# Expert products of a decoder step: from three fp32r products on split weights to plain fp32 products on column tiles

## What is computed

```python
D_MODEL, N_EXPERTS, TOP_K, D_FF_EXPERT = 1024, 8, 2, 3584

def swiglu(h, w_gate_up, w_down):
    a, b = jnp.split(h @ w_gate_up, 2, axis=-1)
    return (jax.nn.silu(a) * b) @ w_down

def moe_swiglu(h, w_router, b_router, w_gate_up, w_down):
    logits = (h @ w_router).astype(jnp.float32) + b_router.astype(jnp.float32)
    top_val, top_idx = lax.top_k(logits, TOP_K)
    top_w = jax.nn.softmax(top_val, axis=-1)
    gates = jnp.sum(jax.nn.one_hot(top_idx, N_EXPERTS) * top_w[..., None], axis=-2)
    y = jnp.zeros_like(h)
    for e in range(N_EXPERTS):
        y = y + gates[..., e:e + 1] * swiglu(h, w_gate_up[e], w_down[e])
    return y
```

## Time and profile before

| | |
|---|---|
| runs of the kernel | 1690.48, 1697.03 and 1693.4 us, median 1693.4 |
| span of the profiled execution, first to last instruction | 1690.0 us |
| TensorE, VectorE, ScalarE busy | 95%, 75%, 64% of the span |
| mean granted clock of TensorE | 0.975 |
| read and written in memory | 522.56 MB and 17.48 MB |

### The profile page before, as it was taken

One profiled execution on the slowest core, in us unless ns is written; L12 is line 12 of the kernel. 1 busy time (PEld: TensorE's weight loads), 2 busy tenths in 40 slices (PEclk: granted clock), 3 DMA queues, 4 the chain that ended last, 5 costly groups with the idle time before them and its releaser, 6 DMA issues.

```text
span 1690.0 us, 25152 instructions
## 1 busy us (share of the span) xinstructions
PE 1603.4 (95%) x9180; PEld 1304.9 (77%) x9180; DVE 1266.3 (75%) x1446; ACT 1074.4 (64%) x1302; POOL 84.2 (5%) x121
## 2 busy tenths in 40 slices
PE   7999899999997888999999999999999999999993
PEld 3983778899896465788788888888888888888883
DVE  4653654454677244899898998998998998998993
ACT  4633444443554443787777877777877777877771
POOL 2011010000024000000000000000000000000001
PEclk9999899999999899999999999999999999999996
DMA  9559578875576987999999999999999999999972
GB/s 348 182 214 352 193 244 290 298 249 182 212 250 242 374 295 271 349 361 368 376 377 376 380 371 378 373 375 376 376 374 378 374 374 383 368 368 386 380 281 103
DMA packets 239603, 540.96 MB, mean 320 GB/s; under 512 B 5931, under 2 KB 28585, under 8 KB 239538
## 3 DMA queue, kind: packets, MB, share of 16 engines
q1 hardware_dynamic: 229202, 504.42, 82.2%
q0 software_dynamic: 9392, 32.39, 5.2%
q10 hardware_dynamic: 944, 3.26, 0.5%
HBM read 522.56 MB, written 17.48 MB: 320 GB/s over the span
## 4 chain that ended last, share of the span: by engine, by line
PE 73%; issue 16%; DVE 4%; DMA 4%; ACT 1%; POOL 0%; SPq 0%; ACTq 0%; DVEq 0%; POOLq 0%
PE psum L780 21%; PE psum L781 21%; PE psum L782 21%; PE psum L699 2%; DMA ring<-in_ada_w 2%; PE psum L1181 1%; DVE w_lo L1722 1%; DMA ring<-in_moe_w_gate_up 1%; PE psum L889 1%; PE psum L692 1%; DVE ring L2061 1%; PE psum L1024 1%; PE psum L1175 1%; PE psum L860 0%; DMA h<-q_scratch 0%
## 5 line engine op out<-in xcount | busy, mean ns | idle before, releaser
L2221 DVE TENSOR_TENSOR w_lo<-ring,w_hi 128x1024 fp32r<-128x1024 f32 x672 | 812.6, 1225 | 79.7 <-ACT w_hi L1643 66.5
L1643 ACT CAST w_hi<-ring 128x1024 fp32r<-128x1024 f32 x672 | 704.8, 1053 | 204.4 <-PE psum L782 186.8
L780 PE MATMUL psum<-w_hi,xe_hi 128*128 128x512 f32 x896 | 359.5, 401 | 3.0 <-DVE w_lo L2221 3.0
L781 PE MATMUL psum<-w_lo,xe_hi 128*128 128x512 f32 x896 | 355.0, 396 | 0.0
L782 PE MATMUL psum<-w_hi,xe_lo 128*128 128x512 f32 x896 | 354.8, 396 | 0.0
L1722 DVE TENSOR_TENSOR w_lo<-ring,w_hi 128x1024 fp32r<-128x1024 f32 (+1 forms) x132 | 161.9, 1236 | 145.8 <-ACT w_hi L1322 145.7
L780 PE MATMUL psum<-hh,w_hi 128*128 128x264 f32 x864 | 254.4, 294 | 16.7 <-DVE w_lo L1722 9.3
L781 PE MATMUL psum<-hl,w_hi 128*128 128x264 f32 x864 | 248.2, 287 | 0.0
L782 PE MATMUL psum<-hh,w_lo 128*128 128x264 f32 x864 | 248.0, 287 | 0.0
L1322 ACT CAST w_hi<-ring 128x1024 fp32r<-128x1024 f32 (+1 forms) x132 | 135.9, 1034 | 106.8 <-PE psum L782 69.0
L780 PEld LDWEIGHTS psum<-w_hi,xe_hi 128*128 128x128 f32 x896 | 169.0, 189 | 42.4 <-DVE w_lo L2221 3.9
(11 more groups left out here) (373 smaller groups left out, 1403.6 us busy)
## 6 DMA issues: line engine op xcount, KB each, us to landing
ring<-in_moe_w_gate_up SPq DMA_DIRECT2D x112, 2048.0 KB, 9.6
ring<-in_moe_w_down SPq DMA_DIRECT2D x56, 2048.0 KB, 9.0
ring<-in_ada_w SPq DMA_DIRECT2D x24, 2048.0 KB, 9.1
ring<-in_ffn_w_gate_up SPq DMA_DIRECT2D x22, 1024.0 KB, 7.7
ring<-in_gla_w_in SPq DMA_DIRECT2D x6, 2048.0 KB, 10.8
ring<-in_kv_ada_w SPq DMA_DIRECT2D x4, 2048.0 KB, 8.9
ring<-in_ffn_w_down SPq DMA_DIRECT2D x4, 2048.0 KB, 8.6
ring<-in_kv_w SPq DMA_DIRECT2D x4, 2048.0 KB, 11.3
```

Source lines behind the costliest of these rows:

```text
L780: eng.matmul(to, wh, ah, start=start, stop=False)
L781: eng.matmul(to, wh, al, start=False, stop=False)
L1643: eng.copy(unit(w_hi, kind, n), quarter(ring[(BASE + j // 4) % RING], kind, j % 4)).then_inc(S["hi_ready"], 1)
L2221: eng.tensor_tensor(unit(w_lo, kind, n), quarter(ring[(BASE + j // 4) % RING], kind, j % 4), unit(w_hi, kind, n), ALU.subtract).then_inc(S ...
```

## The change

The products of the experts are plain fp32 on the loaded tiles. `w_hi`, `w_lo`, `xe_hi`, `xe_lo`, `at_hi` and `at_lo` are no longer used in the sparse branch, nor are the casts and subtractions. `CAP` is 96. A block of 1024 weight columns is four pieces of 256: in three rounds, all 96 tokens meet pieces 0, 1 and 2, on array columns 0 to 63 and 64 to 95; in the same round 32 of the tokens meet piece 3 on array columns 96 to 127. So after three rounds the fourth piece is done too. Its outputs stand in partitions 96 to 127, which the transposes (`turn`), the copy out (`gate_rows`) and the stores (`send_outputs`) take apart again. The ring has six tiles: two in the place of `w_hi` and `w_lo`, one new, and the three old ones. SyncE loads a tile again when TensorE is done with it (`tile_used`). Twelve of the 14 gate and up tiles are now 512 rows x 1024 columns, two stay 1024 x 512. The loop holds two experts (`PAIR`). `y_e` is copied out at the end of an expert instead of at the start of the next, by ScalarE. The dense branch is changed to the new tiles in the same way.

```diff
-CAP = 128
-
-TURN_ROWS_AT, SPLIT_ROWS_AT, GATE_ROWS_AT = 66, 70, 40
+CAP = 96
+ROUNDS = 3
+FULL, REST = 256, 128
+E_RING = 6
+PAIR = 2
...
+PER_BODY = PAIR * PER_E
+UP_TILES = 14
+GROUPS = ((0, 4, FULL), (4, 4, FULL), (8, 4, FULL), (12, 2, REST))
+GROUP_CHUNKS = (8, 8, 8, 4)
+CHUNK0 = (0, 8, 16, 24)
+TURN_AT = {4: 0, 8: 1, 12: 2, 14: 3}
+ROWS_TURN_AT = 18
...
+        e_ring = [stage.enter_context(nc.sbuf_tensor(f"e_ring{i}", [P, TILE], F32)) for i in range(2)]
...
+        e_ring += [st_sb(stage, "e_ring2", [P, TILE])] + [ring[slot] for slot in OLD_SLOTS]
...
-        xe_hi = st_sb(gathered, "xe_hi", [P, KC, CAP], F32R)
-        xe_lo = st_sb(gathered, "xe_lo", [P, KC, CAP], F32R)
-        at_hi = st_sb(gathered, "at_hi", [P, FEC, CAP], F32R)
-        at_lo = st_sb(gathered, "at_lo", [P, FEC, CAP], F32R)
-        silu_e = st_sb(gathered, "silu_e", [CAP, 512])
-        act_e = st_sb(gathered, "act_e", [CAP, 512])
-        y_e = st_sb(gathered, "y_e", [CAP, D])
-        y_g = st_sb(gathered, "y_g", [CAP, D])
+        xe = st_sb(gathered, "xe", [P, KC, CAP])
+        picks = st_sb(gathered, "picks", [P, NE * TT, CAP], F32R)
+        at = st_sb(gathered, "at", [P, FEC, CAP])
+        silu_e = st_sb(gathered, "silu_e", [P, ROUNDS * FULL])
+        act_e = st_sb(gathered, "act_e", [P, ROUNDS * FULL])
+        y_e = st_sb(gathered, "y_e", [P, D])
+        y_g = st_sb(gathered, "y_g", [P, D])
...
+                if i < 12:
+                    s, half = i % 4 // 2, i % 2
+                    c = s * FE + i // 4 * D
+                    src = up[expert, half * 512:(half + 1) * 512, c:c + D].rearrange("(k p) c -> p k c", p=P)
+                elif i < UP_TILES:
+                    c = (i - 12) * FE + 3 * D
+                    return cols8(dst), up[expert, :, c:c + 512].rearrange("(k p) c -> p k c", p=P)
...
+            eng.wait_ge(S["kv_stored"], 16 * 6)
+            eng.wait_ge(S["unit_used"], NU)
+            for j in range(E_RING):
+                if j >= E_RING - RING:
+                    eng.wait_ge(*read_out(*STREAM[LAST_IN[j - (E_RING - RING)]]))
...
-                    value = eng.snap(it * (4 * PER_E) + (NU + 4 * (j - RING) + 4))
-                    eng.wait_ge(S["lo_ready"], value)
...
+                    value = eng.snap(it * PER_BODY + (j - E_RING + 1))
+                    eng.wait_ge(S["tile_used"], value)
...
+            def send_outputs(to, of):
+                to = to[:, :]
+                strip = of[CAP:P, 0:ROUNDS * FULL].rearrange("p (r c) -> p r c", r=ROUNDS)
+                eng.dma_start(to[:, 0:ROUNDS * FULL], of[0:CAP, 0:ROUNDS * FULL]).then_inc(S["y_e_sent"], 16)
+                eng.dma_start(to[:, ROUNDS * FULL:D].rearrange("(r p) c -> p r c", p=STRIP), strip).then_inc(S["y_e_sent"], 16)
...
+                def turn(g):
+                    bank0, width = 3 * (g % 2), GROUPS[g][2]
+                    for c in range(GROUP_CHUNKS[g]):
+                        r, lo = c * P // width, c * P % width
+                        to = pb[bank0 + c // 4][:, c % 4 * CAP:(c % 4 + 1) * CAP]
+                        if r < ROUNDS:
+                            last = eng.transpose(to, act_e[0:CAP, r * width + lo:r * width + lo + P], ident[0:CAP, 0:CAP])
+                            continue
+                        for s in range(ROUNDS):
+                            last = eng.transpose(to[:, s * STRIP:(s + 1) * STRIP], act_e[CAP:P, s * width + lo:s * width + lo + P],
+                                                 ident[CAP:P, CAP:P])
                     last.then_inc(S["turned"], 1)
 
+                def rounds(outs, tokens, j, k, width, first, stop, opens=(0, 1, 2)):
+
+                    for r in range(ROUNDS):
+                        start = first and r in opens
+                        w, rest = expert_cols(j, k, r * width, width), expert_cols(j, k, ROUNDS * width, width)
+                        eng.matmul(outs[r][0:64, :], tokens[:, 0:64], w, start=start, stop=stop, skip_group_check=True)
+                        eng.matmul(outs[r][64:CAP, :], tokens[:, 64:CAP], w, start=start, stop=stop, skip_group_check=True)
+                        last = eng.matmul(outs[r][CAP:P, :], tokens[:, r * STRIP:(r + 1) * STRIP], rest, start=start, stop=stop,
+                                          skip_group_check=True)
+                    return last
+
+                down_outs = [psum[:, (6 * 512 + r * FULL):(6 * 512 + (r + 1) * FULL)] for r in range(ROUNDS)]
...
+                with eng.Fori(0, NE // PAIR) as it:
+                    for e in range(PAIR):
+                        def of(per, n):
+                            return it * (PAIR * per) + (e * per + n)
+
+                        eng.wait_ge(S["xe_act_kept"], of(1, 1))
+                        eng.wait_ge(S["xe_dve_kept"], of(1, 1))
+                        for i in range(PER_E):
+                            j = e * PER_E + i
+                            if i < UP_TILES:
+                                g = min(i // 4, 3)
+                                first, n_tiles, width = GROUPS[g]
+                                if i == first and g == 1:
+                                    eng.wait_ge(S["rows_placed"], 5)
+                                if i == first and g >= 2:
+                                    eng.wait_ge(S["at_act_kept"], of(4, g - 1))
+                                    eng.wait_ge(S["at_dve_kept"], of(3, g - 1))
+                                expert_landed(eng, it, j)
+                                s = (i - first) * 2 // n_tiles
+                                outs = [pb[3 * (g % 2) + r][:, s * FULL:s * FULL + width] for r in range(ROUNDS)]
+                                ks = range(KC) if n_tiles == 2 else range((i - first) % 2 * 4, (i - first) % 2 * 4 + 4)
+                                for n, k in enumerate(ks):
+                                    last = rounds(outs, xe[:, k, :], j, n, width, k == 0, k == KC - 1)
+                            else:
+                                i0 = i - UP_TILES
+                                if i0 == 0:
+                                    eng.wait_ge(S["y_kept_free"], of(1, 1))
+                                    eng.wait_ge(S["at_act_kept"], of(4, 3))
+                                    eng.wait_ge(S["at_dve_kept"], of(3, 3))
+                                if i0 == 6:
+                                    eng.wait_ge(S["at_act_kept"], of(4, 4))
+                                expert_landed(eng, it, j)
+                                for k in range(4):
+                                    c = 4 * i0 + k
+                                    last = rounds(down_outs, at[:, c, :], j, k, FULL, c == 0, c == FEC - 1, opens=(0, 2))
+                            last.then_inc(S["tile_used"], 1)
+                            if i in TURN_AT:
+                                eng.wait_ge(S["gate_up_kept"], of(4, TURN_AT[i] + 1))
+                                turn(TURN_AT[i])
+                            if i == ROWS_TURN_AT:
+                                eng.wait_ge(S["expert_rows"], it * (PAIR * 16) + (e * 16 + 32))
+                                turn_rows()
...
+                with eng.Fori(0, NE // PAIR) as it:
+                    for e in range(PAIR):
+                        def of(per, n):
+                            return it * (PAIR * per) + (e * per + n)
+
+                        for g, (first, n_tiles, width) in enumerate(GROUPS):
+                            eng.wait_ge(S["tile_used"], of(PER_E, first + n_tiles))
+                            if g >= 1:
+                                eng.wait_ge(S["gate_up_kept"], of(4, g))
+                            gates = psum[:, 3 * (g % 2) * 512:3 * (g % 2 + 1) * 512].rearrange("p (r c) -> p r c", r=ROUNDS)
+                            eng.activation(silu_e[:, 0:ROUNDS * width].rearrange("p (r c) -> p r c", r=ROUNDS), gates[:, :, 0:width],
+                                           ACT.Silu).then_inc(S["e_silu"], 1)
+                            eng.wait_ge(S["turned"], of(4, g + 1))
+                            eng.copy(at[:, CHUNK0[g]:CHUNK0[g] + 4, :], pb[3 * (g % 2)][:, 0:4 * CAP]
+                                     .rearrange("p (k c) -> p k c", k=4)).then_inc(S["at_act_kept"], 1)
+                        keep_rows(of(2, 3))
+                        eng.wait_ge(S["tile_used"], of(PER_E, PER_E))
+                        eng.wait_ge(S["y_kept_free"], of(1, 1))
+                        eng.copy(y_e[:, 0:ROUNDS * FULL], psum[:, 6 * 512:6 * 512 + ROUNDS * FULL]).then_inc(S["y_e_kept"], 1)
...
+                keep_rows(2)
+                eng.wait_ge(S["last_spread"], 48)
+                with eng.Fori(0, NE // PAIR) as it:
+                    for e in range(PAIR):
+                        def of(per, n):
+                            return it * (PAIR * per) + (e * per + n)
+
+                        for g, (first, n_tiles, width) in enumerate(GROUPS):
```

(27 more changed lines are left out.)

297 lines of the change are left out of this document (99 added, 198 removed).

## The result

The changed kernel takes 3104.5 us (median of four runs, 3101.8 to 3106.6) where the kernel before takes 1693.2 us (1690.5 to 1697.0) beside it: a ratio of 1.832, 95% interval 1.829 to 1.835. The forecast was 1648 us. The first rival, different widths that don't share the array, had been priced at 3040 us.

What follows compares the result with a forecast made beforehand. TensorE was taken to set the pace, transfers close behind. It starts near 676, plus 3 and 8 x 115.7 us gives 1604.6; the end stage of 38 plus 1 gives a span of 1644, a time of 1648 us (1620 to 1685).

Steps and rivals of the forecast that it cites:

- The first rival: Expert products: the 64-wide product runs alone, the 32-wide pair after it, 1.10 us a round, 3040 us; chance 0.34.
- Part (2): Expert products on TensorE: 64-, 32- and 32-wide tiles work at once, 0.43 us a round, 108.4 us against 117.9 us.
- the exclusion: Expert products: column tiles of different widths don't share the array, 3040 us; chance 0.34.
- the rival's lower end: Expert products, widths not sharing: a change of shape costs 0.09 us, 1.04 us a round, 2905 us at the least.
- part (3): TensorE's transposes: 5.4 us against 3.9, plus 14 changes of tile shape at 0.1 us each, 1.4 us.
- Part (1): VectorE and ScalarE: 88 and 103 us of casts and subtractions per expert go, beside TensorE's work; gain by itself nothing.
- Part (4): Waits added on TensorE for tiles and activations: cost nothing; 4 x 2 us per expert if their cover were gone.
- Parts (5) and (7): Start and end: six loads early, first gather shares the bus, 0 to 3 us; first product 2 us earlier; end plus 1.
- Part (6): Expert weight transfers: 361.7 MB at 386 GB/s, ending at 1588 us; bounds 376 and 395 GB/s.
- the rival's 376: Transfers bind: the bus gives no more than 376 GB/s, so 1662 us; chance 0.13.

Runs made afterwards that it cites:

- strips4: The changed kernel with the 64-wide product split into two 32-wide ones, so each round has four equal column tiles: 1698.7 us, ratio 1.0012.
- pair64: The changed kernel with two 64-wide products a round, the second on the fourth weight piece; products of tokens 64 to 95 with three pieces left out: 1657.3 us.
- halves: The changed kernel's work re-placed: tokens 0 to 63 in paired 64-wide products, 64 to 95 in four 32-wide, one width change a tile: 1683.9 us, ratio 0.9925.
- halves4: The halves kernel with four experts in a loop body in place of two: 1671.6 us, ratio 0.9865.
- only64: The changed kernel with only the 64-wide product of each round, the products on array columns 64 to 127 left out: 1653.9 us.

## Why the prediction was wrong

**Part (2) failed, at "If 64, 32 and 32 do likewise, a round is two steps of 256 columns, 0.43 us".** A round takes 1.13 us. All rows behind that step had tiles of one width: four of 32, or two of 64. They were right for their case; strips4, pair64 and halves run at 0.43 us a round. The step to three widths that differ had no row, and the rows that did hold a change of shape all spoke against it. They were put aside because in each of them something besides the width differed. The forecast was given 0.42 and the exclusion 0.34, on the ground that the strips are "independent streams". The evidence weighed the other way: two groups of rows with a gap at a change of shape, none with two shapes side by side.

The Trainium skill, "TensorEngine Tiling (Array Packing)", section Key Properties, says that a switch of tiling mode empties the engine, where a move to another tile of the same mode doesn't. The runs agree, and for the narrowest case of it: same 128 rows, columns that don't overlap, only the width differs, 0.14 us a switch and no sharing.

**The rival's price** was 1.10 us a round, 290 us a period, 3040 us. Measured are 1.13 us, 297 and 298 us by turns, and 3104 us. The term that was too small is the change of shape: the 1.10 us leave 0.12 us for each of the two beside 4 x 0.215 us, the rival's lower end 0.09, part (3) took 0.1; it is 0.14. 8 x 7.4 us are 59 of the missing 64 us, and the later start gives 3 more.

**Part (1)**, splitting off the path, was right: 7.6 and 6.1 us an expert are left on VectorE and ScalarE, and the time shows no gain from it. **Part (4)** was right: between 900 and 2900 us TensorE waits 3.8 us in all ahead of a product, and for nothing but "issue". The slow pace of the changed kernel could hide a wait, but pair64 and halves at full pace show none either: from 900 to 1600 us they too wait for nothing but "issue".

**Parts (5) and (7)**, the start, were wrong by 5 us in this execution. Six loads are under way by 665 as foreseen (the first at 646.5, the last three from 650.4), and the bus is full at 412 GB/s where it had 248. But "the first gather [...] shares the bus; 0 to 3 us" left out that the rows it gathers must be stored first, over the same bus. The gather is issued at 670.29 instead of 663.53, now released by that store, and takes 7.8 us. That is no more than in the kernel before, where it took between 8.4 and 8.8 us:

```profile
665.26 4.78 issue
670.29 7.78 DMA xe_rows<-h_rows,row_from
678.11 1.55 PE psum L1207 x8
```

The first product starts at 680.49 instead of 677.26, where 2 us earlier was forecast. Not all of the delay is the store: everything ahead of it runs 2.6 us later in this execution (the first copy to `h_tok` at 657.94 instead of 655.32). In pair64, whose code ahead of the experts is the same, that copy is 0.6 us later than before, the gather 5.1 us and the first product, at 678.79, 1.5 us.

**Part (6)**, the transfers, couldn't be seen in the changed kernel (share 0.43). The versions that use the array settle it: 396 GB/s in pair64 and 390 and 392 GB/s in halves4 and halves over experts without a turn. So the bus gives more than the 386 taken, and the rival's 376 was too low.

**Missing from all parts: the code.** The loop before had one block of instructions loaded in 600 us, the new one is loaded in each pass. In the changed kernel that costs 1.2 to 1.4 us a turn. With equal widths it costs 6 to 9 us a turn (3 to 5 us in only64, which has the fewest instructions), and strips4 loses in it and in gaps like it all that fp32 gains: its experts take 122.5 us on average, the kernel before 121.45. The forecast of TensorE's period, 115.7 us, stands between the 114.5 of pair64 and the 116.4 of halves, both without a turn: with equal widths that term holds, and the turns are what the sum lacks.

## What to carry to other kernels

Column tiles of TensorE worked side by side here only when they had one width, 32 or 64 columns: place the work so that a whole block of instructions has one width, and count 0.14 us for each switch beside the part of the array that stands empty. A behaviour shown by rows of equal tiles says nothing of unequal ones; where the only rows of a change of shape show a gap, the forecast should start from the gap. When a change multiplies the instructions of a loop body, as this one does from 1084 records of matmuls and weight loads an expert to 3414, look at the instruction queue of the profile, and unroll further rather than less once the body is loaded anew in each pass anyway.

## What was not expected of the hardware

- Width alone, on columns that don't overlap and with all 128 rows, is enough to keep tiles apart: 1.13 us a round against 0.43, while the two 32-wide products behind the 64-wide one start within 0.01 us of each other.
- A turn of a loop whose body is loaded anew stops TensorE for 4.3 to 5.4 us under a full bus (2.9 to 3.4 us in only64), for 2.6 to 2.8 us with the bus at 0.46, and TensorE goes on 1.7 to 2.0 us after the block of instructions has ended. Then 3 us and more follow at the lower clock, 0.50 to 0.52.
- Four experts in the body cost nothing more than two: 61 blocks of instructions in 600 us against 65, and 116.4 us for an expert without a turn in both.
